# Two norms behind an expert stage folded into one row factor, with a feed-forward and an attention loop reordered

## The reference

```python
def rmsnorm(x, g):
    y = x * rsqrt(mean(x * x) + EPS)
    return y * g
...
# first block
x = x + m @ w_out[l]
h2 = rmsnorm(x, g_ffn[l])
x = x + peer_ffn(h2, w_q[l], sub_keys[l], expert_u[l], expert_v[l])   # 8 heads, 16 experts each, per token
...
x = rmsnorm(x, g_final)
# second block, layer 0
xn = rmsnorm_2(h, norm_mix[0])
q, k, v, g, lr, mq = split_cols(xn @ gla_w_in[0], GLA_SIZES)
log_a = log_sigmoid(lr @ gla_w_gate_up[0] + gla_b_gate[0]) / 16
...
h = h + concatenate([main, mo]) @ w_out[0]
h = h + conv_ffn(rmsnorm_2(h, norm_ffn[0]), w_up[0], conv_w[0], conv_b[0], w_down[0])
# conv_ffn: u = x @ w_up; a depthwise convolution of width 3 over tokens; (silu(a) * b) @ w_down
```

## Time and profile before

| | us |
|---|---|
| median of 3 runs | 1721.08 |
| lowest, highest | 1714.3, 1721.88 |
| the profiled execution | 1721.67 |
| its span | 1719.8 |
| TensorE busy | 1543.5 |
| VectorE busy | 930.0 |
| GpSimd busy | 522.0 |
| ScalarE busy | 404.6 |

### The profile page before, as it was taken

One profiled execution on the slowest core, in us unless ns is written; L12 is line 12 of the kernel. 1 busy time (PEld: TensorE's weight loads), 2 busy tenths in 40 slices (PEclk: granted clock), 3 DMA queues, 4 the chain that ended last, 5 costly groups with the idle time before them and its releaser, 6 DMA issues. The chain is left out here.

```text
span 1719.8 us, 20808 instructions
## 1 busy us (share of the span) xinstructions
PE 1543.5 (90%) x7196; PEld 1128.3 (66%) x7198; DVE 930.0 (54%) x2261; ACT 404.6 (24%) x975; POOL 522.0 (30%) x464
## 2 busy tenths in 40 slices
PE   7999999899777777777779999999999999899998
PEld 6888865454223322223237788899998877799997
DVE  3402566676667767675542632666663134556665
ACT  1110122222222222222124421111122234211112
POOL 2000133334443343444402103454540000345542
PEclk9999999999999999999989999999999989999999
DMA  6448399999999999999943136344444300344441
GB/s 262 148 162 185 124 421 426 427 413 414 427 427 427 427 427 427 426 425 413 427 153 135 45 134 233 118 165 165 146 150 146 123 25 1 147 147 147 157 171 61
DMA packets 56879, 421.56 MB, mean 245 GB/s; under 512 B 6560, under 2 KB 7008, under 8 KB 10752
## 3 DMA queue, kind: packets, MB, share of 16 engines
q0 software_dynamic: 38944, 277.19, 39.6%
q1 hardware_dynamic: 17856, 143.39, 22.9%
HBM read 416.12 MB, written 3.45 MB: 244 GB/s over the span
## 5 line engine op out<-in xcount | busy, mean ns | idle before, releaser
L1659 PE MATMUL wide<-arena 128*128 128x512 f32 x1024 | 473.2, 608 | 121.8 <-ACT arena L541 121.8
L1659 PEld LDWEIGHTS wide<-arena 128*128 128x128 f32 x1024 | 188.0, 191 | 395.4 <-ACT arena L541 201.3
L1111 DVE CUSTOM_DVE_ANT_0 arena<-arena,wide 128x1024 f32<-128x1024 f32 x256 | 312.6, 1221 | 195.0 <-DMA arena<-uv_dram,arena 194.6
L437 POOL DMA_INDIRECT arena<-uv_dram,arena x256 | 259.3, 1013 | 408.6 <-PE wide L1659 284.6
L1496 PE MATMUL bank<-hT,wring 128*128 128x256 f32 (+2 forms) x1008 | 223.5, 383 | 4.7 <-DVE hT L934 3.0
L541 ACT ACTIVATE arena<-arena 128x2 f32<-128x2 f32 (+3 forms) x196 | 66.9, 343 | 616.0 <-DVE arena L1111 440.4
L1496 PEld LDWEIGHTS bank<-hT,wring 128*128 128x128 f32 (+2 forms) x1008 | 182.9, 182 | 42.6 <-issue 7.0
L1308 DVE SCALAR_TENSOR_TENSOR arena<-arena,prm 128x254 f32<-128x254 f32 (+1 forms) x152 | 154.6, 1056 | 61.1 <-ACT arena L541 55.5
L1872 PE MATMUL wide<-arena,wring 128*128 128x256 f32 x704 | 158.6, 379 | 0.0
L1872 PEld LDWEIGHTS wide<-arena,wring 128*128 128x128 f32 x704 | 130.9, 190 | 16.2
L448 POOL TENSOR_TENSOR arena<-arena 128x512 f32<-128x512 f32 x18 | 23.6, 1313 | 356.0 <-ACT arena L541 355.2
(11 more groups left out here) (218 smaller groups left out, 1731.8 us busy)
## 6 DMA issues: line engine op xcount, KB each, us to landing
wring<-ffn_dram SPq DMA_DIRECT2D x44, 1536.0 KB, 6.5
wring<-win_dram SPq DMA_DIRECT2D x16, 1024.0 KB, 4.8
wring<-wout_dram SPq DMA_DIRECT2D x8, 1024.0 KB, 9.3
wring<-wout_dram SPq DMA_DIRECT2D x4, 1280.0 KB, 5.5
wring<-mix_dram SPq DMA_DIRECT2D x4, 1024.0 KB, 4.7
wring<-wqd_dram SPq DMA_DIRECT2D x4, 1024.0 KB, 9.8
arena<-uv_dram,arena POOLq DMA_INDIRECT x256, 12.3
wring<-memkv_dram SPq DMA_DIRECT2D x4, 1024.0 KB, 8.9
```

Of the source, the lines that this page charges most:

```text
L437: pool.indirect_dma_start(out=G[:, n % NBUF, :], out_offset=None, in_=a["uv"], in_offset=bass.IndirectOffsetOnAxis(ap=idx[:, u, r:r + 1], ...
L1111: V.tensor_tensor_reduce(out=G[:, n % NBUF, 0:D], in0=G[:, n % NBUF, 0:D], in1=wide[:, 0:2, :].rearrange("p a b -> p (a b)"), scale=1.0, s ...
L1659: ins = MM(wide[:, 2 + h, :], diag[:, n % 4, e, :], G[:, r % NBUF, D + 512 * h:D + 512 * (h + 1)], start=r % (HEADS * TOPK) == 0, stop=r % ...
```

## The change

It has three parts.

A. The two norms are computed as one factor per token. ScalarE computes once sqrt(g_final² + eps) per feature and squares xT with this scale, so that one mean gives the product of both norms' factors (`both`, `mean_both`, and rstd by `inverse`). gla_lr and gla_qk0 are projected from xT times the constant g_final × norm_mix (`gain0`, `lead`) before the factor is known, and VectorE multiplies both results by it in PSUM. Gains, squares and projections of the first 128 tokens are issued while the experts of the second 128 are still worked on; so glalr and the first slot of glaqk are loaded 28 dots before the end. The last pair of experts is handled one expert at a time, and the transposes of the last sum use wide banks 0 and 1. The g_final norm of xT itself, with its squares on POOL (`squares_fin`), comes behind.

B. In the feed-forward, `seven` puts VectorE's taps and product of the tile before between the joins of this one, and ScalarE keeps the first product ahead of the silu of the tile before. The tap order is turned round.

C. In the NSA loop VectorE issues `nsa_probs` of the next job ahead of `nsa_max` three jobs on.

```diff
-  ("peer_back", 4, DVE_), ("mean_fin", 1, DVE_), ("mean_mix0", 1, DVE_), ("gla_lr", 1, ACT_), ("gla_qk0", 1, ACT_),
-  ("gla_gate", 2, ACT_), ("gla_qk1", 3, ACT_), ("gla_p0", 2, DVE_), ("gla_v0", 1, ACT_), ("gla_mq", 1, ACT_), ("gla_p1", 2, DVE_),
+  ("peer_back", 2, DVE_), ("gla_lr", 1, ACT_), ("mean_mix0", 1, DVE_), ("gla_qk0", 1, ACT_),
+  ("gla_gate", 2, ACT_), ("mean_fin", 1, DVE_), ("gla_qk1", 3, ACT_), ("gla_p0", 2, DVE_), ("gla_v0", 1, ACT_), ("gla_mq", 1, ACT_), ("gla_p1", 2, DVE_),
...
+                sp.wait_ge(dots, TOPK * UNITS - 28)
+            elif name == "glaqk" and slot == 1:
                 sp.wait_ge(dots, TOPK * UNITS - 2)
...
+    def squares_fin(t, adds):
+        T_ = slice(128 * t, 128 * t + 128)
+        pool.wait_ge(added, adds)
+        nc.gpsimd.tensor_tensor(sq_fin[:, :, T_], xT[:, :, T_], xT[:, :, T_], ALU.mult).then_inc(fin_done, 1)
+        for n in range(1, 4):
+            pool.wait_ge(fin_done, 4 * t + n)
+            nc.gpsimd.tensor_tensor(sq_fin[:, 0:2, T_], sq_fin[:, 0:2, T_], sq_fin[:, 2 * n:2 * n + 2, T_], ALU.add)\
+                .then_inc(fin_done, 1)
+    squares_fin(0, 6)
+    squares_fin(1, 8)
...
+            steps(copy(fin[:, 0, :], P("g_final", 0, 8), func=ACT.Square))
+            steps.join()
+            steps(copy(fin[:, 1, :], fin[:, 0, :], func=ACT.Sqrt, bias=eps[:]))
...
+    V.tensor_tensor(fin[:, 2, :], P("g_final", 0, 8), P("norm_mix", 0, 8), ALU.mult)
...
+    def both(t, k):
+        return copy(sq_both[:, k, 128 * t:128 * t + 128], xT[:, k, 128 * t:128 * t + 128], func=ACT.Square,
+                    scale=fin[:, 1, k:k + 1])
...
+            if n == UNITS * PAIRS - 1:
+                for e in range(2):
+                    act.wait_ge(dots, 2 * n + 1 + e)
+                    copy(act2[:, p % 2, e:e + 1], dot[:, k, 2 * p + e:2 * p + e + 1], func=ACT.Gelu).then_inc(gelu, 1)
+                    act.wait_ge(wts, n + 1 + e)
+                    act.wait_ge(v_used, 2 * n - 6)
+                    copy(diag[:, n % 4, e, :], ident, scale=wv[:, k, 2 * p + e:2 * p + e + 1]).then_inc(diags, 1)
+                continue
...
+    act.wait_ge(v_low, 1)
+    copy(peer_o[:, 1, 0:512], wide[:, 2, :]).then_inc(low_out, 1)
     act.preload_act_table(ACT.Sqrt)
-    square(memn[0], xT, added, [7, 7, 8, 8])
-    root("mean_fin")
-    square(sqC, xT, normed, [34, 36, 38, 40])
+    for k in range(KT):
+        act.wait_ge(added, 7 + k // 4)
+        both(1, k).then_inc(sq_done, 1)
     root("mean_mix0")
...
+    b = full("gla_lr")
+    act.wait_ge(scaled0, 1)
+    act.wait_ge(fin_done, 8)
+    copy(glr, b[0:16, 0:S]).then_inc(freed[ACT_], 1)
+    b = full("gla_qk0")
+    act.wait_ge(scaled0, 2)
+    copy(gq[:, 0:2, :], halves(b, DK), scale=float(DK) ** -0.5).then_inc(freed[ACT_], 1)
...
         for j in range(PLAIN, 6):
+            keep_product(j)
+            if j > PLAIN:
+                silu(j - 1, j - 1)
             lin_seven(j, j)
-            silu(j, j)
         with act.Fori(0, (FT - 6) // 4) as i:
             for s in range(4):
...
+        dve.wait_ge(turned_back, n - 1)
+        add_back(n, wide[:, n - 2, :])
+        gain0(n)
+    inverse("mean_mix0")
+    b = full("gla_lr")
+    V.tensor_tensor(b[0:16, 0:S], b[0:16, 0:S], rstd[0:16, :], ALU.mult).then_inc(scaled0, 1)
+    finish(hT, xT, fin[:, 2, :])
+    b = full("gla_qk0")
+    V.tensor_tensor(halves(b, DK), halves(b, DK), rstd[0:DK, :].unsqueeze(1).broadcast_to([DK, 2, S]), ALU.mult).then_inc(scaled0, 1)
     norm("mean_fin", xT, [(xT, "g_final", 0)])
-    dve.wait_ge(normed, 40)
-    norm("mean_mix0", xT, [(hT, "norm_mix", 0)])
...
+    def gain0(n):
+        t, k4 = divmod(n, 2)
+        dve.wait_ge(added, 5 + n)
+        for k in range(4 * k4, 4 * k4 + 4):
+            V.tensor_scalar(xgm[:, k, 128 * t:128 * t + 128], xT[:, k, 128 * t:128 * t + 128], fin[:, 2, k:k + 1], None,
+                            ALU.mult).then_inc(gained0, 1)
...
+        def hidden(j, k):
+            dve.wait_ge(f_silu, j + (k0 + 1))
+            if not isinstance(j, int) or j >= 2:
+                dve.wait_ge(f_down, j + (layer * (FT - 1) - 1))
+            V.tensor_tensor(fh[:, k % 2, :], fsa[:, k % 2, :], fy[:, k % 2, 1, :], ALU.mult).then_inc(f_hid, 1)
+        def far_taps(j, k):
+            dve.wait_ge(f_lin, j + (k0 + 1))
+            for c in range(2):
+                steps(tap(j, k, 0, c))
...
+        def seven(j, k, before=None):
...
+            if before:
+                far_taps(*before)
             dve.wait_ge(kept, n + (m0 + 1))
             join(u2s, 2, b2[:, 0:128], p1s)
             join(u3s, 3, b3[:, 0:128], u2s, after=1)
+            if before:
+                steps.join()
+                tap(*before, 1, 0).then_inc(f_conv, 1)
             join(fu[:, k % 2, 1, 128:256], 4, b4[:, 0:128], u3s, after=2)
             join(u4s, 4, b4[:, 0:128], u2s)
+            if before:
+                steps(tap(*before, 1, 1))
             join(fu[:, k % 2, 1, 0:128], 5, b2[:, 128:256], u3s)
             join(fu[:, k % 2, 0, 0:128], 6, b1[:, 128:256], p1s)
+            if before:
+                steps.join()
+                hidden(*before)
             join(fu[:, k % 2, 0, 128:256], 7, b4[:, 128:256], u4s, after=4)
...
+    nsa_probs(0)
     for J in range(len(NSA)):
-        nsa_probs(J)
+        if J + 1 < len(NSA):
+            nsa_probs(J + 1)
...
+        elif u == HEADS + 2 and p == 1:
+            mean_both(0, begin("mean_mix0"), 4)
+        elif u == UNITS - 1 and p == 2:
+            pe.wait_ge(gained0, 8)
+            lead("gla_lr", begin("gla_lr"), slot("glalr", 0), 16, 0, 0)
+        elif u == UNITS - 1 and p in (4, 6):
+            b = begin("gla_qk0") if p == 4 else bank[GROUP0["gla_qk0"] % 4]
+            lead("gla_qk0", b, slot("glaqk", 0), DK, p // 2 - 2, 0)
...
+    def mean_both(t, b, squares):
+        for k in range(KT):
+            pe.wait_ge(sq_done, squares + t * (k + 1))
+            ins = MM(b[:, 128 * t:128 * t + 128], C("mean_d", 128), sq_both[:, k, 128 * t:128 * t + 128],
+                     start=k == 0, stop=k == KT - 1)
+        return ins
+    def lead(stage, b, w, rows, m, t):
+        for k in range(KT):
+            if t and stage == "gla_lr":
+                pe.wait_ge(gained0, 8 + k + 1)
+            ins = MM(b[0:rows, m * S + 128 * t:m * S + 128 * t + 128],
+                     w[:, (m * KT + k) * rows:(m * KT + k + 1) * rows], xgm[:, k, 128 * t:128 * t + 128],
+                     start=k == 0, stop=k == KT - 1)
+        return ins
...
+    pe.wait_ge(dots, UNITS * TOPK)
+    pe.wait_ge(low_out, 1)
+    back(2, wide[:, 0, :]).then_inc(turned_back, 1)
+    pe.wait_ge(peer_out, 3)
+    back(3, wide[:, 1, :]).then_inc(turned_back, 1)
+    done(lead("gla_lr", bank[GROUP0["gla_lr"] % 4], slot("glalr", 0), 16, 0, 1))
+    done(mean_both(1, bank[GROUP0["mean_mix0"] % 4], 4))
+    for m in range(2):
+        ins = lead("gla_qk0", bank[GROUP0["gla_qk0"] % 4], slot("glaqk", 0), DK, m, 1)
+    done(ins)
...
+    b = begin("mean_fin")
+    pe.wait_ge(fin_done, 8)
+    for k in range(2):
+        ins = MM(b[:, 0:S], C("mean_d", 128), sq_fin[:, k, :], start=k == 0, stop=k == 1)
+    done(ins)
```

More of the change, by code:

```diff
@@ L1662, in _ @@
                     between(u, p)
[L1663 to L1667 removed]
+            pe.wait_ge(dots, UNITS * TOPK)
[8 more added lines that the diff above has]
+            done(ins)
             def gla_qk(stage, i, slot_):
[L1669 removed]
+                done(project(slot("glaqk", slot_), hT, begin(stage, i), rows=DK, norms=None if i else 32))
             def gla_v(i):
@@ L1756, in values @@
                 ins.then_inc(a_o, 1)
-            b = begin("gla_lr")
-            done(project(slot("glalr", 0), hT, b, rows=16, tiles=1, norms=40))
-            gla_qk("gla_qk0", 0, 0)
             pe.wait_ge(freed[ACT_], TAKEN[GROUP0["gla_lr"]])
```

136 lines of the change are left out of this document (72 added, 64 removed).

## The result

| | before | after |
|---|---|---|
| median of 4 runs | 1719.58 us | 1697.3 us |
| lowest, highest | 1714.3, 1721.88 | 1694.28, 1702.75 |
| ratio, with its 95% interval | | 0.9868 [0.9838, 0.9898] |
| the profiled execution | 1721.67 | 1697.9 |
| its span | 1719.8 | 1696.1 |

The change is faster, by 1.3%, where 1691 us was forecast. The kernel before stands at 1719.58 us here, so 22.3 of the forecast's 30.1 us came and 7.8 did not.

What follows compares the result with a forecast made beforehand. TensorE was taken as the bound, busy 90%, with DMA at share 1.00 in the expert stage. Terms -17.6 (norms), -3.3 (feed-forward) and -9.2 (NSA) sum to -30.1, so 1721.1 becomes 1691 us, range 1680 to 1703.

Steps and rivals of the forecast that it cites:

- The saving of 19.6: Behind the expert stage: the remaining gla_qk would start at 893 instead of 912.62, 19.6 us sooner.
- The port penalty: Behind the experts: VectorE's last gains wait for POOL's square on the shared port, up to 2.6 us added.
- the sign that was named for a wrong A: Behind the experts: VectorE's gains or hT with a first instruction over 2 us, or gates waiting for ScalarE.
- The clock, which I expected to fall once: TensorE's clock falls to 1.2 GHz in the gap behind the experts; mean ends at 888.5 if also late, not 884.1.
- +2.0 us: Expert stage: loading glalr and glaqk's first slot early, 0.85 MB at 420 GB/s, lengthens the stage by 2.0 us.
- What it adds on the queues: Costs of the norm change: early loads 2.0 us, early squares and gains nothing, POOL's two DMAs 0 to 0.5.
- This stall goes: Feed-forward tiles: TensorE's wait for VectorE's first join disappears, the join being ready at 2.4 where wanted at 3.55.
- what is late next is the weight path: Feed-forward tiles: weight loads have 6.37 us free against a median 6.5, costing some 0.25 a tile, 9.5 over 38.
- 12.4 less 9.5: Feed-forward layers: 12.4 us of stalls removed, 9.5 returned as waits for weights; forecast as -3.3 us, bounds 0 and -12.4.
- Rival 1: Feed-forward tiles: the weight path is not tight, all 12.4 us go, another 9.1 gained, total 1682 us; chance 0.15.
- the pair before the last: NSA loop: the pair of jobs before the last gains 0.9 us, beside 6.3 for seven pairs and 2.0 elsewhere.
- The slower rival: Feed-forward tiles: VectorE's taps and hidden product collide with POOL's sums, costing 33 us, total 1727; chance 0.04.

Runs made afterwards that it cites:

- after_again: The unaltered change measured once more, in the group of later follow-up runs: 1703.42 us, 0.9893 of the kernel before.
- x_fin_back: The whole change with its new tensor fin allocated behind the arena instead of ahead of it: 1690.45 us, 0.9849 of the kernel before.
- x_pad_256: The change with fin widened from 96 to 256 bytes per partition, still ahead of the arena: 1695.77 us, 0.9842 of the kernel before.
- y_lag_one: The change with each feed-forward tile's down projection one tile behind, not two, and two joins later: 1690.02 us, 0.984 of the kernel before.
- y_gains_first: The change with POOL's squares of the second token tile waiting for VectorE's gains: 0.9863 of the kernel before.

## Why the prediction was right, and where it was wrong

The median (1697.3) lies 6 us above the 1691 and inside the range. Part of that is luck: taken as means over the traces, the parts are worth 16.8 us and not 30.1 (below), which from 1721.1 gives 1704.3, just above the range's end of 1703; the execution profiled first lost 6.8 us less to half clock in the NSA layer than that of the kernel before. Of the forecast's steps:

**Part A, the gain: as forecast.** I had the remaining gla_qk 15.6 us behind the end of the last pair of experts (893 less 877.4); it is 903.27 - 887.51 = 15.8. The saving of 19.6 came as 19.3 in this pair of traces. Two of its terms did not go as told, and against each other. The port penalty came nearly in full (2.2 of up to 2.6 us), and with it the sign that was named for a wrong A, a first gain of over 2 us (2.02). The clock, which I expected to fall once, did not in the profile (1.00 in the stretch from 887 to 903); in after_again it did, and its mean took 2.67 us instead of 2.05. Over all traces part A is worth 16.7: the kernel before took 216.0 us in this stretch, the longest of the five with this code (212.3 to 216.0), and the change 197.0, with two others the shortest of its six; the forecast, made against that one execution, took it for the usual one.

**Part A, the cost: the step that failed.** "+2.0 us" for the loads was right (2.1 to 2.3 measured) and was not all. The sentence under "What it adds on the queues" listed instructions and DMAs, and the change also adds a tensor. Its 96 bytes ahead of the arena cost the gathers 1.4% of their rate, 8.6 us over the stage. Nothing in the rows could price that; the new allocation could have raised the question. The experiments answer it: with the buffers back on a multiple of 256 bytes the change takes 0.9849 and 0.9842 of the kernel before (x_fin_back, x_pad_256), which is 26 and 27 us of the 30 forecast, and beside the second of them the change itself took 7.7 us longer. That x_fin_back's median, 1690.45, is so near to the 1691 is chance, since the kernel before took 1723.24 beside it.

**Part B: right in kind and size.** "This stall goes" and "what is late next is the weight path" are both in the chain, and in many places every second tile pays, as said. -3.3 was forecast and -3.2 is the mean (in this pair of traces -2.1). The forecast's own terms, 12.4 less 9.5, are 2.9 and not 3.3, so the nearness to 3.3 says less than the mean tile: 9.96 us, where 9.95 was named. Rival 1, that the path is not tight, was wrong; y_lag_one shows that the 12.4 us of stalls were really there to be had, since the tiles then take 349.4 us, 12.4 less than the old code's 361.8.

**Part C: right in kind, a little too large.** The period is 6.26 us as worked out, the wait of 2.00 in front of the second turn is gone (the first transposes start at 1373.51 and the first wout1 piece at 1376.94, without a wait between them), and the layer is 7.8 us shorter, not 9.2. By start times the pair before the last gave 0.65 (6.33 to 5.68) for the 0.9 of the sum; the other 1.1 is less than the spread of the layer between kernels with one code (207.1 to 210.3), and stays open.

**The sum.** From the traces' means the terms are 2.3 + 8.6 - 16.7 - 3.2 - 7.8 = -16.8 us; the two measured ratios say -22.7 and -18.4. The second interval, 13 to 24 us, holds the -16.8; the first, 17.5 to 28, just misses it. The sum leaves the clock out, and the two profiled executions of the pair differ by 7 us of half clock in the NSA layer alone (8.5 to 1.7). That the change makes it fall less often was not shown: over all traces that layer lost 3.4 to 10.2 us with the old loop and 1.7 to 15.4 with the new one. The slower rival did not happen: VectorE's two far taps took 2.67 us beside POOL, and no tile waited for its joins.

## What to carry to other kernels

A new tensor moves what is allocated behind it: here the gathers had their full rate only with their buffers on a multiple of 256 bytes, so keep such buffers there, and compare the GB/s of a DMA-bound stage before and after any change, even one that does not touch it. Where a stall is removed, the next path in line can be worked out beforehand from the chain, and here the cure was to free its buffer one tile sooner. And forecast against several executions where the clock moves: one profile's half-clock stretches are not a property of the kernel.

## What the runs showed of the hardware that was not expected

- The rate of gathers of 8 KB rows into SBUF was 427 GB/s where their buffers start at a multiple of 256 bytes and 421 at 96 or 128 bytes past one, in most slices of the stage and in fourteen traces without exception. Loads of the same size into a ring 128 bytes past a multiple were as fast as the gathers beside them, 309 ns a descriptor, and slowed down with them to 313 or 314.
- Four VectorE multiplies of 128 columns took 0.88 us alone and 3.08 beside POOL instructions of 1.89 and 0.78 us.
- In kernels whose feed-forward and NSA layers are the same, TensorE's granted clock fell in different places: in the NSA layer y_gains_first lost 11.9 us to it and the change 1.7. What decides it stays open.
